# A hybrid decoder layer: the residual row of the last stage added on TensorE instead of VectorE

## The chip, the cores and the metric

The kernel runs on one core of a Trainium2 chip. The metric is the device time of one execution in microseconds. A core has TensorE (PE, matrix products into PSUM), VectorE (DVE), ScalarE (ACT), GpSimd (POOL) and SyncE (SP), each with an instruction stream of its own that it works off in order; they wait for one another by semaphores. Transfers run on DMA queues that SP, ACT and POOL issue to.

## The reference

One inference step of a decoder layer on 1024 new prompt tokens, 16 meta tokens and 8 sampled tokens: linear attention and windowed attention side by side, an output projection with a LayerNorm, and then a mixture of experts with a second LayerNorm. Only the last lines matter for the change:

```python
h1 = layer_norm(ALPHA * h + merged @ w_out, ln1_g, ln1_b)
f = hier_moe(h1...)                  # each token: two experts, weights w_top
#   segment_sum(out[dest] * w_s[:, None])
h2 = layer_norm(ALPHA * h1 + f, ln2_g, ln2_b)

def layer_norm(x, g, b):
    mu = mean(x); var = mean((x - mu) ** 2)
    return (x - mu) * rsqrt(var + LN_EPS) * g + b
```

So for each token the last stage takes its two expert rows, weighs and adds them, adds the row of h1 times ALPHA = 2^0.25, and normalises the sum.

## The kernel before, in words

The tokens stand in NB = 9 blocks of 128 rows and D = 1024 columns. The stages before (projections, attention, output projection, routing) end with the experts: a loop over 32 tiles of 128 gathered rows, each with its expert's weights loaded, split into a high and a low part and multiplied (L1915 to L1917). ACT writes each result tile (yb) to obuf_dram (L1333, L1335).

The last stage begins when the last of these stores has landed. All engines run through blocks 0 to 8 in order, each with its own code:

- POOL gathers for each block the two expert rows of each token, ya and yc, from obuf_dram (L1006), 18 indirect DMAs. Later it adds ln2_b to each block (L1012).
- ACT makes for each block two diagonal matrices dg, the identity scaled by the token's two weights (L1351, L1352). Later, for each block, it makes the reciprocal root of the variance (L1019, L1021) and the normalised row (L1358).
- PE multiplies dg with ya and yc, which weighs each row and adds both in PSUM (L2269, L2270): four products of 512 columns a block. Block b writes the two banks 2*(b % 4) and the next, so PSUM holds four blocks. Before block b it waits for f_z of block b-4 (L2266).
- DVE, in f_sum(b), forms zz = ALPHA * h1 + PSUM (L1887, it sets f_z), then the statistics of zz (L555, L556, L558). f_scale(b-1) multiplies the block before by ln2_g (L1899), and f_mean(b) makes the shift for ACT (L1894). This is the order in its stream.
- SP loads h1 of blocks 0 to 5 into h1l long before, of blocks 6 to 8 into h1e once the experts' memory is free (both L808), and stores each finished block.

h1l and h1e hold the rows of h1; PS is PSUM; zz and st2 have two buffers each. upto(n) is the value that a step's semaphore has once step n is done; f_h[b] is the semaphore of block b's load of h1, f_y[b % 4] that of its gathers, f_dg that of the diagonal matrices (it shares its semaphore with n_whi), n_xn that of the normalised rows, n_hg that of the scaled ones.

Of the kernel before, what the change touches and what calls it, by code (L numbers as in the profile page):

```python
# [31 lines left out]
ACT = mybir.ActivationFunctionType  # L32
ALU = mybir.AluOpType
# [3 lines left out]
P = 128  # L37
# [3 lines left out]
NB = 9  # L41
# [6 lines left out]
ALPHA = 2.0 ** 0.25  # L48
# [18 lines left out]
def upto(n):  # L67

    return n + 1 + CREDIT


def build(nc, A, R):
    ctx = ExitStack()

    def sem(name):
        return ctx.enter_context(nc.semaphore(name))
# [3 lines left out]
    def ssem(name):  # L80
        s = sem(name)
        step_sems.append(s)
        return s
# [13 lines left out]
    def sb(stack, name, shape, dt=F32):  # L97
        return stack.enter_context(nc.sbuf_tensor(name, shape, dt))

    both = ctx  # L100
    PS = ctx.enter_context(nc.psum_tensor("PS", [P, 8, 512], F32))
    ident = sb(both, "ident", [P, P])
# [50 lines left out]
    bias = sb(sW, "bias", [P, 2, HPG, 2 * P])  # L153
# [125 lines left out]
    h1l = sb(sE, "h1l", [P, NB - 3, D])  # L279
# [4 lines left out]
    sF = ExitStack()  # L284
    ya = sb(sF, "ya", [P, NB, D])
    yc = sb(sF, "yc", [P, NB, D])
    h1e = sb(sF, "h1e", [P, 3, D])
    zz = [sb(sF, f"zz{s}", [P, D]) for s in range(2)]
    st2 = [sb(sF, f"st2{s}", [P, 16]) for s in range(2)]
    dg = sb(sF, "dg", [P, NB, 2, P])  # L290
    ln2_g = sb(sF, "ln2_g", [P, D])
    ln2_b = sb(sF, "ln2_b", [P, D])
    sF.close()
# [16 lines left out]
    n_sa = ssem("n_sa")  # L310
    n_st = ssem("n_st")
# [3 lines left out]
    n_xn = ssem("n_xn")  # L315
    n_hg = ssem("n_hg")
# [118 lines left out]
    f_h = ((c_in, 32), (c_rin, 64), (c_brow, 16), (b_gn, 160), (b_gk, 32), (s_in, 64), (s_shift, 32), (s_win, 144), (o_small, 96))  # L435
    f_dg, f_s = n_whi, n_wlo
    f_base = 21
    f_z = ssem("f_z")

    BF = lambda t: t.bitcast(F32)  # L440
    most, rest = slice(1, NB), slice(0, 1)
# [16 lines left out]
    def wait_apart(eng, s, value):  # L458


        if not isinstance(value, int):
            value = eng.to_reg(value)
        eng.wait_ge(c_id, 3)
        eng.wait_ge(s, value)
# [88 lines left out]
    def stats(dve, z, t, s_a, s_b, n):  # L553

        dve.bn_stats(t[:, 0:6], z[:, 0:512])  # L555
        dve.bn_stats(t[:, 6:12], z[:, 512:1024]).then_inc(s_a, 1)  # L556
        wait_apart(dve, s_a, n)
        dve.bn_aggr(t[:, 12:14], t[:, 0:12]).then_inc(s_b, 1)  # L558
# [457 lines left out]
    def _(act):  # L1016
        def rsqrt(src, tmp, dst, s_a, s_b, n, scale=1.0):

            act.activation(tmp, src, ACT.Ln, bias=eps_c[0:src.shape[0], :], scale=scale).then_inc(s_a, 1)  # L1019
            act.wait_ge(s_a, n)  # L1020
            act.activation(dst, tmp, ACT.Exp, scale=-0.5).then_inc(s_b, 1)  # L1021
# [328 lines left out]
        def f_diag(b):  # L1350
            act.activation(dg[:, b, 0], ident[:], ACT.Copy, scale=wts[:, b, 0:1])  # L1351
            act.activation(dg[:, b, 1], ident[:], ACT.Copy, scale=wts[:, b, 1:2]).then_inc(f_dg, 1)  # L1352

        def f_norm(b, s):
            act.wait_ge(n_st, upto(2 * NB + b))
            rsqrt(st2[s][:, 13:14], st2[s][:, 14:15], st2[s][:, 15:16], n_ln, n_rs, upto(2 * NB + b))
            act.wait_ge(n_nm, upto(2 * NB + b))
            act.activation(zz[s][:], zz[s][:], ACT.Identity, bias=st2[s][:, 14:15], scale=st2[s][:, 15:16]).then_inc(n_xn, 1)  # L1358

        for b in range(NB):  # L1360
            f_diag(b)
        for b in range(NB):
            f_norm(b, b % 2)
# [3 lines left out]
    def _(dve):  # L1367
# [513 lines left out]
        def f_sum(b, s):  # L1881

            dve.wait_ge(f_s, f_base + b + 1)
            dve.wait_ge(f_h[b][0], f_h[b][1] + 16)
            dve.wait_ge(n_hg, upto(2 * NB + b - 2))
            q = 2 * (b % 4)
            dve.scalar_tensor_tensor(zz[s][:], h1l[:, b] if b < NB - 3 else h1e[:, b - NB + 3], ALPHA, PS[:, q:q + 2].rearrange("p a n -> p (a n)"),  # L1887
                                     ALU.mult, ALU.add).then_inc(f_z, 1)
            dve.wait_ge(f_z, upto(b))
            stats(dve, zz[s], st2[s], n_sa, n_st, upto(2 * NB + b))  # L1890

        def f_mean(b, s):
            dve.wait_ge(n_rs, upto(2 * NB + b))
# [3 lines left out]
        def f_scale(b, s):  # L1897
            dve.wait_ge(n_xn, upto(2 * NB + b))
            dve.tensor_tensor(ya[:, b], zz[s][:], ln2_g[:], ALU.mult).then_inc(n_hg, 1)  # L1899

        f_sum(0, 0)
        f_mean(0, 0)
        dve.wait_ge(f_small, 32)
        for b in range(1, NB):
            f_sum(b, b % 2)
            f_scale(b - 1, 1 - b % 2)
            f_mean(b, b % 2)
# [4 lines left out]
    def _(pe):  # L1912
# [188 lines left out]
        for a in range(8):  # L2101
            if a >= 2:
                pe.wait_ge(act_s, a - 1)
            for m in range(4):
                g, n = (4 * a + m) // NS, (4 * a + m) % NS
# [20 lines left out]
        for g in range(G):  # L2126
            for h in range(HPG):
                c = (g % 2) * DV + h * HD
# [131 lines left out]


        pe.wait_ge(m_ya, upto(2 * iters + 1))
        for b in range(NB):
            pe.wait_ge(f_dg, f_base + b + 1)
            pe.wait_ge(f_y[b % 4], 32 * (b // 4 + 1))
            pe.wait_ge(f_z, upto(b - 4))  # L2266
            for half in range(2):
                c = slice(half * 512, half * 512 + 512)
                pe.matmul(PS[:, 2 * (b % 4) + half], dg[:, b, 0], ya[:, b, c], start=True, stop=False)  # L2269
                last = pe.matmul(PS[:, 2 * (b % 4) + half], dg[:, b, 1], yc[:, b, c], start=False, stop=True)  # L2270
            last.then_inc(f_s, 1)

    ctx.close()

# [36 lines left out]
```

## Time and profile before

| | |
|---|---|
| median of 3 runs | 1925.24 us (1923.21 to 1931.18) |
| the profiled execution | 1924.17 us, its span 1922.0 us |
| PE, DVE, ACT, POOL busy | 1731.5, 1219.6, 884.9, 306.0 us |
| last expert product ends | about 1850.5 us |
| first product of the last stage | 1866.78 us |
| DVE's first step in it | 1872.95 us |

The span is the time from the first to the last instruction in one profiled execution. Times in a timeline are us from its start. PEclk is the TensorE clock that was granted: 1.00 is 2.4 GHz and 0.50 is 1.2 GHz. A product of f32 operands runs as two passes, so it appears as two weight loads and two matmuls in the trace. Of the 1922 us the last stage takes the last 70 or so.

### The profile page before, as it was taken

The numbers are of one execution on the slowest core, as the hardware profiler recorded it, in microseconds if no ns is written. First come the engines' busy times: TensorE is split into PE (matmuls) and PEld (weight loads), VectorE is DVE, ScalarE is ACT, GpSimd is POOL, SyncE is SP. The second block draws the span as 40 slices with busy tenths as digits, with TensorE's granted clock in tenths as the row PEclk, the third lists the DMA queues.
The fourth block names the chain that finished last, engine by engine and source line by source line (L and its number), as shares of the span: only waits on it lengthen the run. The fifth ranks groups of instructions, "written<-read, shape, count | busy, mean of one in ns | idle before, by whom it ended". The sixth has DMA issues, their size and how long they took to land. (4 is left out here: it accounts for less than half of the span.)

```text
span 1922.0 us, 28799 instructions
## 1 busy us (share of the span) xinstructions
PE 1731.5 (90%) x9022; PEld 1461.6 (76%) x9022; DVE 1219.6 (63%) x1695; ACT 884.9 (46%) x1446; POOL 306.0 (16%) x386
## 2 busy tenths in 40 slices
PE   2899999899999999999978899359999999999955
PEld 2899999788788878878846787348888888888832
DVE  5510110577778767867753333859889988988917
ACT  2432221344445435433411122237787778778723
POOL 1200000122312322232210111010001000010025
PEclk9999999899999999999967899579999999999978
DMA  6486521434433433432269324369999999999854
GB/s 212 147 253 198 177 82 50 146 102 131 142 106 124 135 121 101 158 102 86 84 204 326 122 98 187 119 242 388 413 415 411 415 413 412 416 414 411 328 215 194
DMA packets 183313, 422.90 MB, mean 220 GB/s; under 512 B 24977, under 2 KB 123169, under 8 KB 158425
## 3 DMA queue, kind: packets, MB, share of 16 engines
q1 hardware_dynamic: 129776, 321.93, 45.2%
q0 software_dynamic: 20048, 69.06, 10.2%
q10 hardware_dynamic: 33408, 30.94, 4.6%
q8 instruction: 39, 0.64, 0.1%
q14 instruction: 42, 0.34, 0.1%
HBM read 354.83 MB, written 78.55 MB: 225 GB/s over the span
## 5 line engine op out<-in xcount | busy, mean ns | idle before, releaser
L1786 DVE TENSOR_TENSOR wm_lo<-raw,wm_hi 128x2048 fp32r<-128x2048 f32 x192 | 434.2, 2290 | 72.0 <-ACT wm_hi L1293 70.9
L1293 ACT CAST wm_hi<-raw 128x2048 fp32r<-128x2048 f32 x192 | 363.4, 1911 | 72.8 <-PE PS L1917 44.5
L1915 PE MATMUL PS<-w_hi,hT_hl 128*128 128x512 f32 (+1 forms) x584 | 232.9, 399 | 11.9 <-DMA hT_hl<-hl_dram 8.5
L1916 PE MATMUL PS<-w_lo,hT_hl 128*128 128x512 f32 (+1 forms) x584 | 227.0, 389 | 0.0
L1917 PE MATMUL PS<-w_hi,hT_hl 128*128 128x512 f32 (+1 forms) x584 | 226.6, 388 | 0.0
L1915 PE MATMUL PS<-wm_hi,xT_hi 128*128 128x512 f32 x512 | 203.9, 398 | 2.9 <-DVE xT_lo L1848 2.9
L1917 PE MATMUL PS<-wm_hi,xT_lo 128*128 128x512 f32 x512 | 200.8, 392 | 0.0
L1916 PE MATMUL PS<-wm_lo,xT_hi 128*128 128x512 f32 x512 | 200.5, 392 | 0.0
L1955 PE MATMUL PS<-xa_hi,wn 128*128 128x384 f32 x480 | 161.8, 337 | 0.2
L1957 PE MATMUL PS<-xa_hi,wn 128*128 128x384 f32 x480 | 161.1, 336 | 0.0
L1956 PE MATMUL PS<-xa_lo,wn 128*128 128x384 f32 x480 | 161.1, 336 | 0.0
L1408 DVE TENSOR_TENSOR wn<-nraw,wn 128x1024 fp32r<-128x1024 f32 x20 | 24.5, 1226 | 180.3 <-ACT wn L1040 180.3
L1915 PEld LDWEIGHTS PS<-w_hi,hT_hl 128*128 128x128 f32 x584 | 110.7, 190 | 35.1 <-issue 13.1
L1917 PEld LDWEIGHTS PS<-w_hi,hT_hl 128*128 128x128 f32 x584 | 110.6, 189 | 24.9
L1916 PEld LDWEIGHTS PS<-w_lo,hT_hl 128*128 128x128 f32 x584 | 111.0, 190 | 21.7
L1561 DVE RECIPROCAL Rt<-Et 128x512 f32<-128x512 f32 x36 | 120.7, 3353 | 3.2
L1189 ACT ACTIVATE Sc<-Sc,nmx 128x256 f32<-128x256 f32 (+1 forms) x144 | 69.9, 487 | 109.1 <-DVE nmx L1537 72.5
L1915 PEld LDWEIGHTS PS<-wm_hi,xT_hi 128*128 128x128 f32 x512 | 97.2, 190 | 22.8 <-DVE xT_lo L1848 2.8
L1917 PEld LDWEIGHTS PS<-wm_hi,xT_lo 128*128 128x128 f32 x512 | 96.8, 189 | 21.0
L1916 PEld LDWEIGHTS PS<-wm_lo,xT_hi 128*128 128x128 f32 x512 | 97.0, 189 | 19.6
L1061 ACT COPY ev<-PS 128x384 f32<-128x384 f32 x60 | 28.7, 479 | 171.8 <-PE PS L1957 168.6
L1915 PE MATMUL PS<-wm_hi,hT_hi 128*128 128x512 f32 x256 | 103.0, 403 | 4.5 <-DVE hT_lo L1866 4.5
(340 smaller groups left out, 3387.4 us busy)
## 6 DMA issues: line engine op xcount, KB each, us to landing
raw<-in_w_gate SPq DMA_DIRECT2D x64, 1024.0 KB, 6.9
raw<-in_w_up SPq DMA_DIRECT2D x64, 1024.0 KB, 7.9
raw<-in_w_down SPq DMA_DIRECT2D x64, 1024.0 KB, 8.5
hT_hl<-hl_dram POOLq DMA_DIRECT2D x70, 512.0 KB, 5.4
braw<-in_w_in SPq DMA_DIRECT2D x16, 1024.0 KB, 6.3
obuf_dram<-yb ACTq DMA_DIRECT2D x32, 512.0 KB, 8.2
nd_dram<-ev ACTq DMA_DIRECT2D x72, 192.0 KB, 2.7
nd<-nd_dram SPq DMA_DIRECT2D x36, 384.0 KB, 3.8
```

Source lines behind the costliest of these rows:

```text
L1061: act.copy(ev[k % 3][:], PS[:, 3 + m % 3, 0:T3]).then_inc(n_ev, 1)
L1189: act.activation(Sc[:, h, lo:], Sc[:, h, lo:], ACT.Exp, bias=nmx[:, h:h + 1], accum_out=su[:, h:h + 1])
L1293: act.copy(wm_hi[:, j], raw[:, j]).then_inc(m_hi[j // 4], 1)
L1408: dve.tensor_tensor(lo[:], nraw[r % 3][:], BF(hi[:]), ALU.subtract).then_inc(n_wlo, 1)
L1561: dve.reciprocal(Rt[:], Et[:, 1:3]).then_inc(b_R, 1)
L1786: dve.tensor_tensor(wm_lo[:, j], raw[:, j], BF(wm_hi[:, j]), ALU.subtract).then_inc(m_lo[j // 4], 1)
L1915: pe.matmul(out, x_hi, w_hi_, start=start, stop=False)
L1916: pe.matmul(out, x_hi, w_lo_, start=False, stop=False)
L1917: return pe.matmul(out, x_lo, w_hi_, start=False, stop=stop)
L1955: pe.matmul(out, hi[:, k], xa_hi[:, tc, k], start=(k == 0), stop=False)
L1956: pe.matmul(out, hi[:, k], xa_lo[:, tc, k], start=False, stop=False)
L1957: last = pe.matmul(out, lo[:, k], xa_hi[:, tc, k], start=False, stop=(k == KC - 1))
```

## The change

ALPHA times the row is added by PE: a third diagonal matrix da, the identity times ALPHA, is multiplied with h1l or h1e, ahead of the two products with dg in the same PSUM banks. The rows of blocks 0 to 3 are multiplied ahead of all products with dg; the row of block b+4 directly behind those of block b, after a wait for ACT's normalised row of block b (n_xn). DVE's combination L1887 and its semaphore go. The statistics read PSUM, and so does ACT's normalisation, which then writes zz.

```diff
+    da = sb(sF, "da", [P, P])
...
             act.wait_ge(n_nm, upto(2 * NB + b))
-            act.activation(zz[s][:], zz[s][:], ACT.Identity, bias=st2[s][:, 14:15], scale=st2[s][:, 15:16]).then_inc(n_xn, 1)
-
+            act.wait_ge(n_hg, upto(2 * NB + b - 2))
+            act.activation(zz[s][:], PS[:, 2 * (b % 4):2 * (b % 4) + 2].rearrange("p a n -> p (a n)"), ACT.Identity, bias=st2[s][:, 14:15], scale=st2[s][:, 15:16]).then_inc(n_xn, 1)
+
+        act.activation(da[:], ident[:], ACT.Copy, scale=ALPHA).then_inc(f_dg, 1)
...
             dve.wait_ge(f_s, f_base + b + 1)
-            dve.wait_ge(f_h[b][0], f_h[b][1] + 16)
-            dve.wait_ge(n_hg, upto(2 * NB + b - 2))
             q = 2 * (b % 4)
-            dve.scalar_tensor_tensor(zz[s][:], h1l[:, b] if b < NB - 3 else h1e[:, b - NB + 3], ALPHA, PS[:, q:q + 2].rearrange("p a n -> p (a n)"),
-                                     ALU.mult, ALU.add).then_inc(f_z, 1)
-            dve.wait_ge(f_z, upto(b))
-            stats(dve, zz[s], st2[s], n_sa, n_st, upto(2 * NB + b))
+            stats(dve, PS[:, q:q + 2].rearrange("p a n -> p (a n)"), st2[s], n_sa, n_st, upto(2 * NB + b))
...
         pe.wait_ge(m_ya, upto(2 * iters + 1))
+        def rows(b):
+            pe.wait_ge(f_h[b][0], f_h[b][1] + 16)
+            if b >= 4:
+                pe.wait_ge(n_xn, upto(2 * NB + b - 4))
+            src = h1l[:, b] if b < NB - 3 else h1e[:, b - NB + 3]
+            for half in range(2):
+                pe.matmul(PS[:, 2 * (b % 4) + half], da[:], src[:, half * 512:half * 512 + 512], start=True, stop=False)
+
+        pe.wait_ge(f_dg, f_base + 1)
+        for b in range(4):
+            rows(b)
         for b in range(NB):
-            pe.wait_ge(f_dg, f_base + b + 1)
+            pe.wait_ge(f_dg, f_base + b + 2)
             pe.wait_ge(f_y[b % 4], 32 * (b // 4 + 1))
-            pe.wait_ge(f_z, upto(b - 4))
             for half in range(2):
                 c = slice(half * 512, half * 512 + 512)
-                pe.matmul(PS[:, 2 * (b % 4) + half], dg[:, b, 0], ya[:, b, c], start=True, stop=False)
+                pe.matmul(PS[:, 2 * (b % 4) + half], dg[:, b, 0], ya[:, b, c], start=False, stop=False)
                 last = pe.matmul(PS[:, 2 * (b % 4) + half], dg[:, b, 1], yc[:, b, c], start=False, stop=True)
             last.then_inc(f_s, 1)
+            if b + 4 < NB:
+                rows(b + 4)
```

PE's stream before, at the start of the last stage; each row is one product of 512 columns, with the semaphores that it waits for (n_whi is that of dg):

```order
L2269 MATMUL PS<-ya,dg 128x512 [waits f_y0,f_z,n_whi,m_ya]
L2270 MATMUL PS<-yc,dg 128x512
L2269 MATMUL PS<-ya,dg 128x512
L2270 MATMUL PS<-yc,dg 128x512
L2269 MATMUL PS<-ya,dg 128x512 [waits f_z,f_y1,n_whi]
L2270 MATMUL PS<-yc,dg 128x512
```

PE's stream of the changed kernel, from the last row product of blocks 0 to 3 to the first products of block 1 (b_gk is that of the load of block 4 of h1):

```order
L2266 MATMUL PS<-h1l,da 128x512
L2276 MATMUL PS<-ya,dg 128x512 [waits f_y0,n_whi]
L2277 MATMUL PS<-yc,dg 128x512
L2276 MATMUL PS<-ya,dg 128x512
L2277 MATMUL PS<-yc,dg 128x512
L2266 MATMUL PS<-h1l,da 128x512 [waits n_xn,b_gk]
L2266 MATMUL PS<-h1l,da 128x512
L2276 MATMUL PS<-ya,dg 128x512 [waits f_y1,n_whi]
L2277 MATMUL PS<-yc,dg 128x512
```

A block's products now have two row products behind them that wait for n_xn, ahead of the next block's. The same follows blocks 1 to 4.

DVE's stream before, for block 1:

```order
L1887 SCALAR_TENSOR_TENSOR zz<-h1l,PS 128x1024 [waits c_rin,n_hg,n_wlo,f_small]
L555 BN_STATS st<-zz 128x6 [waits f_z]
L556 BN_STATS st<-zz 128x6
L558 BN_AGGR st<-st 128x2 [waits n_sa,c_id]
L1899 TENSOR_TENSOR ya<-zz,ln_g 128x1024 [waits n_xn]
L1894 SCALAR_TENSOR_TENSOR st<-st 128x1 [waits n_rs]
```

and in the changed kernel (n_wlo is PE's f_s):

```order
L555 BN_STATS st<-PS 128x6 [waits n_wlo,f_small]
L556 BN_STATS st<-PS 128x6
L558 BN_AGGR st<-st 128x2 [waits n_sa,c_id]
L1896 TENSOR_TENSOR ya<-zz,ln_g 128x1024 [waits n_xn]
L1891 SCALAR_TENSOR_TENSOR st<-st 128x1 [waits n_rs]
```

The combination is gone, and the statistics wait for PE themselves; the rest stands in the same order.

## Rows read from the trace of the kernel before

**Rows 1.** The page, busy time: us (share of the span) xinstructions.

```profile
PE 1731.5 (90%) x9022; PEld 1461.6 (76%) x9022; DVE 1219.6 (63%) x1695; ACT 884.9 (46%) x1446; POOL 306.0 (16%) x386
```

**Rows 2.** The chain that ended last, 1845 to 1922 us: start, us, what.

```profile
1856.48 10.06 DMA yc<-obuf_dram,ridx
...
1872.95 1.23 DVE zz L1887
1876.57 1.23 DVE zz L1887
...
1880.65 1.23 DVE zz L1887
...
1905.10 1.23 DVE zz L1887
```

**Rows 3.** Timeline of PE, last stage: start, us, engine line, idle before and releaser.

```profile
1866.78 2.04 PE L2269 MATMUL PS<-ya,dg 128*128 128x512 f32 x2 [16.23 <-DMA yc<-obuf_dram,ridx]
1868.62 1.91 PE L2270 MATMUL PS<-yc,dg 128*128 128x512 f32 x2
...
1871.62 1.02 PE L2270 MATMUL PS<-yc,dg 128*128 128x512 f32 x2
1872.48 1.02 PE L2269 MATMUL PS<-ya,dg 128*128 128x512 f32 x2
```

**Rows 4.** Timeline of DVE and ACT, blocks 0 and 1.

```profile
1874.20 0.69 DVE L555 BATCH_NORM_STATS2 st<-zz 128x6 f32<-128x512 f32 x1
...
1876.59 1.24 ACT L1358 ACTIVATE zz<-zz,st 128x1024 f32<-128x1024 f32 x1 [0.23 <-DVE st L1894]
...
1877.83 0.70 DVE L555 BATCH_NORM_STATS2 st<-zz 128x6 f32<-128x512 f32 x1
...
1879.22 0.21 DVE L558 BATCH_NORM_AGGREGATE st<-st 128x2 f32<-128x12 f32 x1
...
1879.35 1.17 DVE L1899 TENSOR_TENSOR ya<-zz,ln_g 128x1024 f32<-128x1024 f32 x1
...
1880.62 1.24 ACT L1358 ACTIVATE zz<-zz,st 128x1024 f32<-128x1024 f32 x1 [0.63 <-DVE st L1894]
```

**Rows 5.** Stretches: length, busy PE, PEld, DVE, ACT, POOL, PEclk, DMA, GB/s.

```profile
1838.80:1843.10 4.30, 0.00 (x0) 0.00 (x0) 3.82 (x3) 2.71 (x3) 0.00 (x0) 1.00 0.13 53
1843.90:1847.30 3.40, 3.40 (x9) 2.61 (x9) 0.00 (x0) 0.00 (x0) 0.00 (x0) 0.50 0.00 0
1850.70:1854.10 3.40, 0.00 (x0) 0.00 (x0) 0.00 (x0) 2.18 (x2) 0.00 (x0) 1.00 0.38 154
1854.30:1866.70 12.40, 0.00 (x0) 0.00 (x0) 0.00 (x0) 5.36 (x18) 7.49 (x8) 0.50 0.85 322
1866.80:1871.20 4.40, 4.40 (x6) 1.82 (x7) 0.00 (x0) 0.00 (x0) 2.80 (x3) 0.50 1.03 412
```

**Rows 6.** Groups by form that read PSUM, on ACT and DVE: busy, mean ns.

```profile
L1333 ACT COPY yb<-PS 128x1024 f32<-128x1024 f32 x32 | 32.6, 1019 | 9.1 <-PE PS L1917 9.1
L1548 DVE COPY Pt<-PS 128x512 f32<-128x512 f32 x36 | 24.8, 690 | 51.5 <-PE PS L2036 51.5
```

**Rows 7.** Timeline, the end: block 8 on DVE and POOL.

```profile
1906.36 0.69 DVE L555 BATCH_NORM_STATS2 st<-zz 128x6 f32<-128x512 f32 x1
...
1910.42 2.13 DVE L1899 TENSOR_TENSOR ya<-zz,ln_g 128x1024 f32<-128x1024 f32 x1 [1.31 <-ACT zz L1358]
1912.63 2.34 POOL L1012 TENSOR_TENSOR ya<-ya,ln_b 128x1024 f32<-128x1024 f32 x1 [1.16 <-DVE ya L1899]
```

**Rows 8.** The first dg on ACT (timeline), and the loads of h1 (line L808).

```profile
1854.48 0.40 ACT L1351 ACTIVATE dg<-ident,wts 128x128 f32<-128x128 f32 x1 [1.06 <-DMA obuf_dram<-yb]
...
L808 SPq DMA_DIRECT2D h1l<-h_dram x6: 340/433/1077, 1214.6 to 1216.9; - x6
L808 SPq DMA_DIRECT2D h1e<-h_dram x3: 424/432/772, 1855.3 to 1856.3; - x3
```

**Rows 9.** Waits, 1866 to 1915 us: total us, times, longest.

```profile
PE PS L2269 <- DMA yc<-obuf_dram,ridx: 16.2, 1, 16.2
```

## What I predict, and how it is worked out

> **What bounds the kernel now.** I read the page first, then the chain of waits over the last 75 us, then the timelines of PE, DVE and ACT in it. The page shows PE busy for 90% of the span [rows 1], but nearly all of that is the projections and the experts, and the change touches none of it. What decides here is the last stage, after the last expert product at 1850.5 us. The chain [rows 2] shows what ends last in it: the gather of yc lands 10.06 us after its issue began at 1856.48 (1866.54), PE does block 0, and from 1872.95 on every step of the chain is on DVE. The combination of a block (L1887) starts at 1872.95, 1876.57, 1880.65 and so on to the ninth at 1905.10, so 4.08 us apart from block 1 on. PE is not late there: from 1872.48 it issues a product of 512 columns every 0.86 us in two passes of 0.43 [rows 3], four to a block, 3.44 us, less than DVE's 4.08, and it runs ahead by up to four blocks of PSUM.
>
> **What the change does to a block.** On DVE it takes away L1887, 1.23 us of those 4.08 [rows 2]; what is left is 2.85. On PE it adds two products for the scaled row, so 6 products, 12 passes, 12 x 0.43 = 5.16 us a block instead of 3.44. For blocks 0 to 3 these are done ahead of the gathers. For blocks 4 to 8 they stand in PE's stream right behind the products of blocks 0 to 4, and with them a new wait: the row of block b+4 overwrites the banks that ACT's normalisation of block b now reads, so it waits for that normalisation. Before, PSUM was free once L1887 had read it, and the wait (f_z) stood four blocks later than the products that filled the bank. Now the wait for block b's normalisation stands directly behind block b's own products. Behind the waiting row are queued the products of block b+1, whose gathers are long in. DVE waits for those, and ACT and POOL for DVE. So five times the last stage goes round a loop in which nothing overlaps.
>
> **The loop, step by step, at the full clock.**
> - From the start of a block's statistics to the end of its normalisation: in block 1 from 1877.83 to 1880.62 + 1.24 = 1881.86, 4.03 us; in it the aggregate and DVE's scale of block 0 (1.17, ahead of the mean in DVE's stream) [rows 4]. In block 0, with no scale between, 1874.20 to 1877.83, 3.63 us. Both engines now read PSUM. For ACT the nearest rows are its copies of 128x1024 from PSUM at 1.02 us against 1.24 for this one out of SBUF; for DVE a copy of 128x512 from PSUM has 0.69 us [rows 6], as the statistics of 512 have [rows 4]. So I take 0.22 off: 3.81 and 3.41. Bounds: no saving, or 0.22 as taken.
> - The end of ACT to PE's first pass: 0.24, as from the landing at 1866.54 to the first product at 1866.78 [rows 2, 3].
> - Two row products and four of the next block: 12 passes from one another at 0.43, 5.16, plus 0.16 that the last pass lasts beyond its 0.43 (1.02 for two).
> - PE's end to DVE's start: 1871.62 + 1.02 = 1872.64 to 1872.95, 0.31 [rows 2, 3].
>
> That makes 3.81 + 0.24 + 5.16 + 0.16 + 0.31 = 9.68 us for a block that took 4.08.
>
> **The clock.** In such a loop PE stands still for 3.81 + 0.24 + 0.31, 4.4 us, in each round. The trace has one pause of that length in the stage before: none busy from 1838.8 to 1843.1, at the full clock, and then 3.4 us of work at a granted clock of 0.50, which is 1.2 GHz, from 1843.9 to 1847.3. After 3.4 us of standing (1850.7 to 1854.1) it also fell to 0.50, stayed there through the wait for the gathers, and for 4.4 us of work after it [rows 5]. A slow stretch of 3.4 us does 1.7 us of work, so it costs 1.7; I take one such stretch for each round: 11.4 us. The bounds are none (9.68) and the whole burst at 0.50: a product then takes 1.71 us instead of 0.86, as the one at 1868.62 with its two passes of 0.85 [rows 3], so the round takes about 15.0.
>
> The Trainium skill, in "TensorE: Matmul & The Clock Gate", section "HAM oscillation — how this bites in real kernels", says that short bursts of matmuls with waits between them lose the full clock in every wait and start each burst at the low one. The pause at 1838.8 agrees, with 0.50 for 3.4 us behind it. Taken so far that the whole burst is slow, it is the rival "slow throughout" below.
>
> **The start.** The products of the rows of blocks 0 to 3 need da, one more copy on ACT ahead of dg, 0.40 us from 1854.48 [rows 8], and h1l, whose loads are issued by 1216.9 [rows 8]. They run from about 1855.1: 16 passes, 6.9 us at the full clock (1862.0), 13.8 at 0.50 (1868.9). The clock fell at 1854.1, and in the kernel before it came back after 4.4 us of work [rows 5]; so they end near 1864 and are hidden by the gathers, which land at 1866.54. Block 0's products then take 7 x 0.43 + 0.59 to the end of the last pass at the full clock and give DVE its start at 1866.78 + 3.60 + 0.31 = 1870.7; at 0.50 as before, 1872.95. I take 1871.5. The statistics start there, with no L1887 ahead: before, 1874.20 [rows 4]. This is all that the change wins at the start, 2.7 us. The loads of h1e (3, 9.4 to 11.5 us to landing, issued by 1856.3 [rows 8]) are in before the row of block 6 is wanted.
>
> **The end.** Behind block 5 no rows are left, and PE paces at 3.44 a block, DVE's 2.85 being less: three blocks, 10.3 us. From the statistics of block 8 to the end of the span it is 1922.0 - 1906.36 = 15.64; in it is DVE's last scale, which took 2.13 beside POOL's addition, POOL's last addition from 1912.63, and the store [rows 7]. All this stays; ACT's 0.22 comes off: 15.42.
>
> **The sum.** 1871.5 + (11.4 - 0.4) + 4 x 11.4 = 1928.1 for the start of block 5; + 10.3 = 1938.4; + 15.4 = 1953.8, against a span of 1922.0. The profiled execution took 1924.17, 2.17 beyond its span, so 1956.0; it lay 1.07 under the median of 1925.24, which is less than the spread of the runs. I predict 1956, 1.6% slower. Nothing else costs: SP's and POOL's streams are the same, and the dg of block 0 comes 0.3 us later in a wait of 12 us.
>
> **The rivals.**
> - Full clock throughout: the loop is there, but pauses of 4.4 us with 5.2 of work between don't lose the clock. For it: more than half of each round is work, and no row shows such a mixture repeated. Against it: the two falls to 0.50 after 4.3 and 3.4 us without work [rows 5]. Time: 1870.7 + 5 x 9.68 - 0.4 + 10.3 + 15.4 = 1944.4, so 1946.6.
> - Slow throughout: the clock does not come back inside a burst. For it: 4.4 us of work at 0.50 after the long wait [rows 5], nearly a burst. Against it: the 3.4 us stretch, after which PE had 1.00. Time: 1872.95 + 5 x 15.0 - 0.4 + 10.3 + 15.4 = 1973.3, so 1975.4.
> - The wait is not felt (the other side): the rows find their bank free when PE comes to them, because something holds PE back by as much anyway. Place: PE at the row of block 4. It decides from the point where the products of block b+1 would start more than 4.4 us after block b's, thus if gathers came that far apart. Price: then PE's own work paces, 5 x 5.16 + 3 x 3.44 = 36.1 from 1871.5, plus 15.4: 1923.0, so 1925.2, no change. Against it: PE waited for a gather once in this stage, before block 0 [rows 9]. If the rows cost PE nothing at all: 1870.7 + 8 x 3.44 + 15.4 = 1913.6, so 1915.8, the best that the change could do, 0.5% faster.
>
> In the same page of the Trainium skill, the section "Architectural detail: the array is 16× 32×32, not 1× 128×128" says that PE's queue may pull a weight load ahead of matmuls in flight. If that reached past the waiting row, it would hide 0.2 us a round at most; the products themselves would still stand behind it. No row here shows either.
>
> **How the numbers follow.** Forecast 0.63, full clock 0.17, slow throughout 0.15, the wait not felt 0.05. The forecast's own range is 1951 to 1964 (one to one and a half slow stretches, and the bounds of the start). The range takes in the full-clock case and two thirds of the way to the slow one: 1945 to 1969. What a measurement tells from no change is 0.5%, 9.6 us: slower means over 1934.9, which all cases but the last give, 0.95; the same 0.04; faster 0.01.
>
> **What would show it.** In the profile after: PE idle five times for about 4.4 us at the row products, with ACT's normalisation as the releaser; DVE's first statistics 11 to 12 us apart over blocks 0 to 5 and about 3.4 over 5 to 8; ACT's normalisation near 1.02; the clock at 0.50 for a part of each burst; eight row products done before the gathers land. Wrong would be: statistics evenly 5.2 us apart (no wait felt), 9.7 (full clock) or 15 (slow), or a time below 1935.

## The result

| | median, us | runs | ratio to before |
|---|---|---|---|
| before, at the time | 1924.22 | 4 | |
| changed | 1959.22 (1954.91 to 1964.01) | 4 | 1.0192 [1.0154, 1.0230] |

The change costs 1.9% by the ratio, 35 us between the medians. The forecast was 1956, 1.6% slower, with 1945 to 1969 for the range. The profiled execution of the changed kernel took 1960.57 with a span of 1958.7.

### The profile page after: what moved, and what is told of

The parts are those of the page before. It is cut to its first block and busy times, and to the rows that moved or that the text cites. A ratio compares the mean times of both kernels' runs of the same rounds, so it can differ in the third digit from the quotient of the medians.

```text
span 1958.7 us, 28867 instructions
## 1 busy us (share of the span) xinstructions
PE 1764.8 (90%) x9058; PEld 1476.6 (75%) x9058; DVE 1209.2 (62%) x1686; ACT 884.5 (45%) x1447; POOL 306.4 (16%) x386
```

## The profile after

Waits of the changed kernel from 1866 to 1955 us (us in total, times, longest). Before, PE waited in this stage only once, for a gather [rows 9]:

```profile
DVE st L555 <- PE PS L2277: 76.7, 9, 29.3
...
PE PS L2266 <- ACT zz L1359: 20.7, 5, 4.3
...
PE PS L2276 <- DMA yc<-obuf_dram,ridx: 2.0, 1, 2.0
```

The second row is the loop: five waits of the row products (L2266) for ACT's normalisation, 20.7 us. DVE's waits for PE are the other side of it.

Timeline of PE, the first two rounds and the last of the five, to answer to [rows 3]:

```profile
1855.90 10.01 PE L2266 MATMUL PS<-h1l,da 128*128 128x512 f32 x16 [4.34 <-issue]
1867.92 1.40 PE L2276 MATMUL PS<-ya,dg 128*128 128x512 f32 x2 [2.01 <-DMA yc<-obuf_dram,ridx]
1869.12 1.91 PE L2277 MATMUL PS<-yc,dg 128*128 128x512 f32 x2
...
1872.27 1.02 PE L2277 MATMUL PS<-yc,dg 128*128 128x512 f32 x2
1877.17 3.75 PE L2266 MATMUL PS<-h1l,da 128*128 128x512 f32 x4 [3.88 <-ACT zz L1359]
1880.72 1.78 PE L2276 MATMUL PS<-ya,dg 128*128 128x512 f32 x2
...
1884.06 1.02 PE L2277 MATMUL PS<-yc,dg 128*128 128x512 f32 x2
1889.33 3.52 PE L2266 MATMUL PS<-h1l,da 128*128 128x512 f32 x4 [4.25 <-ACT zz L1359]
...
1924.13 3.75 PE L2266 MATMUL PS<-h1e,da 128*128 128x512 f32 x4 [4.19 <-ACT zz L1359]
```

The 16 passes of the early rows take 10.0 us and end 2.0 us ahead of the gathers: hidden, as the second row's wait shows. Then PE stands for 3.9 to 4.25 us ahead of each burst of rows and products. The four passes of a block's two row products take 3.5 to 3.75 us, about twice the 1.88 of the full clock (row_late, below).

Timeline of DVE and ACT, one round (block 1), to answer to [rows 4]:

```profile
1885.18 0.70 DVE L555 BATCH_NORM_STATS2 st<-PS 128x6 f32<-128x512 f32 x1 [9.39 <-PE PS L2277]
...
1886.71 1.17 DVE L1896 TENSOR_TENSOR ya<-zz,ln_g 128x1024 f32<-128x1024 f32 x1
...
1887.98 1.20 ACT L1359 ACTIVATE zz<-PS,st 128x1024 f32<-128x1024 f32 x1 [0.63 <-DVE st L1891]
...
1896.32 0.70 DVE L555 BATCH_NORM_STATS2 st<-PS 128x6 f32<-128x512 f32 x1 [8.37 <-PE PS L2277]
```

From 1885.18 to 1887.98 + 1.20 = 1889.18 are 4.00 us, and PE starts 0.15 later. The first statistics of the nine blocks start at 1873.43, 1885.18, 1896.32, 1908.71, 1919.98, 1932.48, 1935.92, 1939.35 and 1942.78: rounds of 11.75, 11.14, 12.39, 11.27 and 12.50, then 3.44, 3.43 and 3.43. Before it was 4.08 a block.

Stretches of the changed kernel, pauses and bursts in turn (length, busy PE, PEld, DVE, ACT, POOL, PEclk, DMA, GB/s), to answer to [rows 5]:

```profile
1885.20:1889.30 4.10, 0.00 (x0) 0.00 (x1) 2.65 (x5) 1.70 (x3) 1.27 (x1) 0.97 0.56 224
1889.40:1896.30 6.90, 6.88 (x12) 2.73 (x12) 0.00 (x0) 0.00 (x0) 0.97 (x1) 0.78 0.03 5
1896.40:1900.40 4.00, 0.00 (x0) 0.00 (x0) 2.58 (x5) 1.70 (x3) 1.30 (x1) 0.86 0.00 0
1900.50:1908.70 8.20, 8.17 (x12) 3.22 (x12) 0.00 (x0) 0.00 (x0) 0.94 (x1) 0.66 0.16 64
```

Twelve passes take 6.9 us in one burst and 8.2 in the next, for 5.2 at the full clock. The granted clock is at one of its two levels at any moment, so a mean of 0.78 or 0.66 is a burst that begins at 0.50 and ends at 1.00: the row products at its head last 3.5 to 3.75 us, the products with dg at its end 1.02.

The times of one kernel spread by up to 14 us (row_late: 1922.32 to 1936.03), so I use a second measure of the traces beside the times: the length of the last stage, from the first product with dg to the start of POOL's last addition. Before it is 1912.63 - 1866.78 = 45.9 us [rows 3, 7], after 1949.30 - 1867.92 = 81.4. The difference of 35.5 is the whole loss. The kernel before ran again beside the experiments: its median was 1927.61 beside the first four and 1927.88 beside the next three, and their ratios are to those runs.

## Experiments

The theory: PE stands because the row of block b+4 waits, in order, for the normalisation of block b, behind block b's own products; the pause costs by itself, and again by the low clock after it. The rivals: the ten added products cost; the reads of PSUM cost; the low clock is the whole cost.

### The same products, moved (row_late)

```diff
         for b in range(NB):
+            if b >= 4:
+                rows(b)
             pe.wait_ge(f_dg, f_base + b + 2)
...
             last.then_inc(f_s, 1)
-            if b + 4 < NB:
-                rows(b + 4)
```

> The changed kernel with one thing moved: the row product of block b (b = 4 to 8) stands directly ahead of block b's own products instead of behind block b-4's. Same 54 products, same waits by value. The wait theory: the normalisation of block b-4 is done by then, so PE never stops; DVE's first statistics come 3.4 us apart for blocks 1 to 3 and 5.2 for blocks 4 to 8, 36 us in all from block 0 to block 8 instead of 69.4, and the time falls by 33 us to about 1926. Rival, the added products (or reading PSUM) cost by themselves: the time stays near 1950 to 1959.

Measured: 1926.75 median, ratio to before 1.0004 [0.9983, 1.0024]. Timeline of PE, blocks 3 to 5:

```profile
1877.96 1.02 PE L2279 MATMUL PS<-yc,dg 128*128 128x512 f32 x2
1878.82 1.88 PE L2266 MATMUL PS<-h1l,da 128*128 128x512 f32 x4
1880.54 1.02 PE L2278 MATMUL PS<-ya,dg 128*128 128x512 f32 x2
...
1883.97 1.88 PE L2266 MATMUL PS<-h1l,da 128*128 128x512 f32 x4
```

No pause is left, all at the full clock, and a block takes 1883.97 - 1878.82 = 5.15 us. From the first statistics (1868.82) to those of block 8 (1904.78) are 36.0 us. Before they were 1906.36 - 1874.20 = 32.2 [rows 4, 7], so this takes 3.8 us longer; 1.9 of them come back at the start, where the statistics begin 5.5 us after the first product with dg instead of 7.4. The last stage is 1911.05 - 1863.32 = 47.7 us, 1.9 more than before. So with every added product and every read of PSUM in place, 1.9 of the 35.5 us are left, and the place of the rows costs 81.4 - 47.7 = 33.7. Even with no pause the full change gains nothing.

### The wait without the products (wait_only)

This kernel leaves ALPHA * h1 out of blocks 4 to 8.

```diff
-            for half in range(2):
+            for half in range(2 if b < 4 else 0):
                 pe.matmul(PS[:, 2 * (b % 4) + half], da[:], src[:, half * 512:half * 512 + 512], start=True, stop=False)
...
-                pe.matmul(PS[:, 2 * (b % 4) + half], dg[:, b, 0], ya[:, b, c], start=False, stop=False)
+                pe.matmul(PS[:, 2 * (b % 4) + half], dg[:, b, 0], ya[:, b, c], start=(b >= 4), stop=False)
```

> The changed kernel without the row products of blocks 4 to 8 (their rows of h1 are left out of the sum), but with their waits in the same places. The wait theory: PE still stops for block b's normalisation behind block b; a round is shorter only by its two products, 1.7 us (at the full clock) of 11.8, so five times 1.7 to 2.6: 1946 to 1951. Rival, the added products cost: it falls to the time of the kernel before, about 1924.

Measured: 1951.58, 0.6 us above the range that I gave, ratio 1.0126 [1.0089, 1.0162]; last stage 1941.14 - 1871.48 = 69.7 us, 11.7 less than the changed kernel. The wait without its products makes 24 of the 35.5 us. Waits, 1870 to 1945 us:

```profile
PE PS L2276 <- issue: 20.5, 5, 4.2
```

The five pauses add up to 20.5 us beside 20.7, though the trace names no releaser for them here. The 11.7 us are more than five times 1.7 (8.6), which the ten products take at the full clock. The other 3.1 are slow work that is gone. The clock didn't fall in every pause here. Timeline of PE, the first burst and the head of the fourth:

```profile
1880.68 1.10 PE L2276 MATMUL PS<-ya,dg 128*128 128x512 f32 x2 [3.84 <-issue]
1881.62 1.02 PE L2277 MATMUL PS<-yc,dg 128*128 128x512 f32 x2
...
1883.33 1.02 PE L2277 MATMUL PS<-yc,dg 128*128 128x512 f32 x2
...
1907.59 2.05 PE L2276 MATMUL PS<-ya,dg 128*128 128x512 f32 x2 [4.14 <-issue]
```

The first burst stands behind a pause of 3.84 us and ran wholly at the full clock (granted clock 1.00); the fourth, behind 4.14 us, had a mean of 0.57. Why one pause loses the clock and another of nearly its length doesn't, no run here settles.

### PE kept at work in the pause (warm)

nul is a matrix of zeros, so its products add 0 to banks that are already being summed, and the result is unchanged.

```diff
+        act.activation(nul[:], ident[:], ACT.Copy, scale=0.0)
         act.activation(da[:], ident[:], ACT.Copy, scale=ALPHA).then_inc(f_dg, 1)
...
             if b + 4 < NB:
+                for half in (0, 1, 0, 1):
+                    pe.matmul(PS[:, 2 * ((b + 1) % 4) + half], nul[:], h1l[:, 0, half * 512:half * 512 + 512], start=False, stop=False)
                 rows(b + 4)
```

> The changed kernel with four extra products by a matrix of zeros (they add 0 to the next block's banks) ahead of each of the five waits, so that PE works in the 4.3 us in which it otherwise stands: 3.4 us of work at the full clock. The clock theory: the 2.0 us by which a round is longer than its steps at the full clock (11.8 measured, 9.8 from the steps) is the low clock after each pause; with PE busy the rounds shrink to about 9.8 and the time falls by 10 to about 1949. Rival, the low clock doesn't come from the pause, or zeros don't count as work: no change in the clock, and the extra products take 6.9 us at 0.50, so the rounds grow to 14 and the time to 1970.

Measured: 1952.14, ratio 1.0131 [1.0092, 1.0170]; last stage 1939.64 - 1869.78 = 69.9 us, 11.5 less. Three of its rounds as stretches (columns as above), and the wait in them:

```profile
1878.70:1888.30 9.60, 8.82 (x20) 3.72 (x20) 2.66 (x5) 1.66 (x4) 3.74 (x4) 1.00 1.03 410
1888.30:1897.90 9.60, 8.82 (x20) 3.72 (x20) 2.66 (x5) 1.73 (x4) 2.44 (x2) 1.00 0.10 35
1897.90:1907.50 9.60, 8.82 (x20) 3.72 (x20) 2.66 (x5) 1.73 (x4) 2.37 (x2) 1.00 0.14 56
```

```profile
1893.90 3.60 PE L2283 MATMUL PS<-h1l,nul 128*128 128x512 f32 x8
1898.25 1.95 PE L2268 MATMUL PS<-h1e,da 128*128 128x512 f32 x4 [0.75 <-ACT zz L1360]
```

With the clock at 1.00 a round is 9.6 us. The products by zeros kept the clock up. So of the 81.4 - 45.9 = 35.5 us, the low clock after the pauses is 11.5, a third; PE works longer and the kernel gets faster. The other two thirds, 24 us, are the serial loop at the full clock: five rounds of 9.6 in place of 4.08, less what the start and the last three blocks (3.44 in place of 4.08) give back.

### The wait in the kernel before (before_wait)

```diff
             pe.wait_ge(f_z, upto(b - 4))
+            if 1 <= b <= 5:
+                pe.wait_ge(n_xn, upto(2 * NB + b - 1))
```

> The kernel before with nothing but a wait added on PE: the products of blocks 1 to 5 wait for the normalisation of the block ahead of them. No added product, no read of PSUM. The wait theory: a round is 1.2 + 4.0 + 0.2 + 3.4 + 0.5 = 9.4 us at the full clock and about 11.1 with one slow stretch, in place of 4.08, five times: 1951 to 1959. Rival, the products or the reads of PSUM make the loss: close to 1924.

Measured: 1963.97, ratio 1.0197 [1.0160, 1.0233], last stage 1952.02 - 1869.41 = 82.6 us. Without a single added product and with the statistics out of SBUF, the wait alone makes the whole loss. It came out 5 us above the upper end that I gave; 3.4 of them are the kernel before, at 1927.61 in this series and 1924.22 when I worked out the range. Waits, 1869 to 1955 us:

```profile
PE PS L2271 <- ACT zz L1358: 21.9, 4, 5.5
```

The fifth pause, ahead of block 1, is 5.3 us; the trace puts it down to a gather, but PE starts 0.14 us after ACT's first normalisation ends (1880.50 and 1880.36). A pause is longer than the changed kernel's, since DVE's combination stands in it. That makes 6.1 us of the difference to wait_only, where the wait cost 24; another 3.8 are the start and the last three blocks, which are as slow here as before (7.3 us to the first statistics, 4.08 a block). Blocks 1 to 3 start their combination at 1885.93, 1898.13 and 1909.35, 12.2 and 11.2 apart, more than the 11.1 that one slow stretch for each round gives.

### One block later (row_one_later)

```diff
             last.then_inc(f_s, 1)
-            if b + 4 < NB:
-                rows(b + 4)
+            if b and b + 3 < NB:
+                rows(b + 3)
```

> The changed kernel with the row products of block b+4 behind the products of block b+1 instead of block b's: one block later. The wait theory: the normalisation of block b ends 4.0 us after its statistics begin, and a block's products take 3.4, so only the first of the five waits still shows (0.5 us or so), and the time is that of the version with the rows directly ahead of their block, 1927 (ratio 1.00), 32 us under the changed kernel. Rival, what that version gained was distance from the gathers or from ACT's queue, so one block is not enough: the waits stay for a part, and the time lies near the middle, 1940.

Measured: 1930.28, ratio 1.0023 [1.0009, 1.0037]; last stage 1916.63 - 1868.06 = 48.6 us. Timeline of PE, the first two rows in the stream:

```profile
1877.31 1.95 PE L2266 MATMUL PS<-h1l,da 128*128 128x512 f32 x4 [0.45 <-ACT zz L1359]
...
1882.54 1.88 PE L2266 MATMUL PS<-h1l,da 128*128 128x512 f32 x4
```

One wait of 0.45 is left of five. Moving each row by one block gives back 32.8 of the 33.7 us of last stage that moving it as far as it goes gives. The stage is 2.7 us longer than before; the ratio says 0.23% slower, with 0.09 to 0.37% for its interval (1.7 to 7 us).

### Only the rows that are free (early_rows_only)

Rows of blocks 0 to 3 as in the changed kernel; blocks 4 to 8 combined on DVE as before.

```diff
+    ON_PE = (0, 1, 2, 3)
...
+            if b in ON_PE:
+                stats(dve, PS[:, q:q + 2].rearrange("p a n -> p (a n)"), st2[s], n_sa, n_st, upto(2 * NB + b))
+                return
...
+            dve.scalar_tensor_tensor(zz[s][:], h1l[:, b] if b < NB - 3 else h1e[:, b - NB + 3], ALPHA, PS[:, q:q + 2].rearrange("p a n -> p (a n)"),
+                                     ALU.mult, ALU.add).then_inc(f_z, 1)
+            dve.wait_ge(f_z, upto(b - 4))
+            stats(dve, zz[s], st2[s], n_sa, n_st, upto(2 * NB + b))
```

> Rows of blocks 0 to 3 on PE, done in the wait for the gathers, with statistics and normalisation out of PSUM; blocks 4 to 8 on DVE as before, with no row product in PE's stream. If DVE is the only bound left in blocks 0 to 3: 1.2 us less for each and one less at the start, about 4 us less than before (ratio 0.998). If DVE's scale and POOL's addition of ln2_b can't run at once (in the version with late rows one scale lasted 3.33 us beside POOL's 2.36), a block can't be shorter than 1.17 + 2.35 = 3.5 us once POOL adds, and 1 us is left (ratio 0.9995).

Measured: 1925.44, ratio 0.9990 [0.9973, 1.0006], not told from before; last stage 1914.20 - 1870.38 = 43.8 us, 2.0 shorter than before, between the two cases that I gave. What came between shows in the timeline of POOL and DVE:

```profile
1884.48 4.67 POOL L1014 TENSOR_TENSOR ya<-ya,ln_b 128x1024 f32<-128x1024 f32 x2
1885.91 4.33 DVE L1907 TENSOR_TENSOR ya<-zz,ln_g 128x1024 f32<-128x1024 f32 x1
1890.16 0.15 DVE L1902 SCALAR_TENSOR_TENSOR st<-st 128x1 f32<-128x1 f32 x1
1890.32 2.37 POOL L1014 TENSOR_TENSOR ya<-ya,ln_b 128x1024 f32<-128x1024 f32 x1 [1.17 <-DVE ya L1907]
1890.37 1.22 DVE L1895 SCALAR_TENSOR_TENSOR zz<-h1l,PS 128x1024 f32<-128x1024 f32 x1
```

POOL had the first two blocks to add one behind the other. A scale of 1.17 us took 4.33: it began during the first addition and ended 1.09 us after the second (1889.15). The combination L1895, with one operand in PSUM, ran beside POOL's next one in its 1.22.

### The last row too, and zeros ahead of the start (early_rows_and_last)

```diff
+    ON_PE = (0, 1, 2, 3, 8)
...
         for b in range(4):
             rows(b)
+        for half in (0, 1) * 1:
+            pe.matmul(PS[:, half], nul[:], h1l[:, 0, half * 512:half * 512 + 512], start=False, stop=False)
...
+            if b >= 4:
+                if b in ON_PE:
+                    rows(b)
```

> As the version with early rows only, and the row of block 8 on PE too, directly ahead of its products, where PE is ahead of DVE; and two products by zeros between the last early row and the gathers, so that PE doesn't stand for 2 us there. Expected: block 0's products at the full clock, 1.7 us earlier than without them, and DVE's last combination gone (1.2 us): 2 to 4 us less than before (ratio 0.998 to 0.999), the best of all versions. Rival: POOL's additions, which can't run beside DVE's scales, set the end: then neither shows, and it is the time of the version before it.

Measured: 1923.89, ratio 0.9983 [0.9967, 0.9999]; last stage 1912.03 - 1868.78 = 43.3 us, 2.6 shorter than before. It has the lowest median of all versions, by less than 0.2%; against early_rows_only its stage is 0.5 us shorter, and the times don't tell the two apart. The start is at the full clock:

```profile
1866.84 1.88 PE L2290 MATMUL PS<-h1l,nul 128*128 128x512 f32 x4
1868.78 1.10 PE L2301 MATMUL PS<-ya,dg 128*128 128x512 f32 x2
```

DVE's first statistics start at 1872.58, 3.8 us after the first product with dg; in the changed kernel it was 1873.43 - 1867.92 = 5.5. That the zeros did this isn't shown: early_rows_only has none, its PE stood for 1.6 us, and its start was at the full clock too, with the statistics (1874.18) 3.8 us after the first product:

```profile
1870.38 1.10 PE L2297 MATMUL PS<-ya,dg 128*128 128x512 f32 x2 [1.61 <-DMA yc<-obuf_dram,ridx]
```

The 1.7 us that I expected from the zeros, against the version with early rows only, did not come.

### POOL's addition cut short (short_pool_add)

This is early_rows_and_last with one more edit. It leaves ln2_b out of 1016 of the 1024 columns.

```diff
-            pool.tensor_tensor(ya[:, b], ya[:, b], ln2_b[:], ALU.add).then_inc(n_h, 1)
+            pool.tensor_tensor(ya[:, b, 0:8], ya[:, b, 0:8], ln2_b[:, 0:8], ALU.add).then_inc(n_h, 1)
```

> The version with early rows and the last one, with POOL adding ln2_b to 8 of the 1024 columns of each block only (the bias is left out for the rest). If POOL's 2.35 us additions hold up DVE's scales: the scale that lasted 4.33 us falls to 1.17 and the last one from 2.1 to 1.17, and from the first product with dg to the start of POOL's last addition it takes 39.1 us instead of 43.25. Rival, the long scales are something else (the gathers' traffic, or ACT reading PSUM at the same time): they stay, and the stage is not shorter.

Measured once: 1914.62 beside 1930.14 of the kernel before, a pair too few to weigh by its times; last stage 1905.22 - 1866.29 = 38.9 us, for 39.1 expected. The line of DVE's scale, count, duration ns min/median/max, first in the version with the full addition, then in this one:

```profile
L1909 DVE TENSOR_TENSOR ya<-zz,ln_g x9: 1171/1171/4328, 1877.5 to 1909.8; 128x1024 f32<-128x1024 f32 x9
```

```profile
L1909 DVE TENSOR_TENSOR ya<-zz,ln_g x9: 1171/1172/1226, 1875.0 to 1903.9; 128x1024 f32<-128x1024 f32 x9
```

No scale is held any more, and the stage is 4.4 us shorter than with the full addition. So in the versions with early rows it is POOL's addition that eats most of what DVE saves.

## Why the prediction was right

The steps, each with what it measured:

- The place of the wait. Right: five pauses with ACT's normalisation as the releaser. row_late, which moves only that place, takes 33.7 us of the stage away, and before_wait, which adds only the wait, makes a loss of that size.
- The round at the full clock, 9.68. Measured 9.6 in warm, where the clock held. Three terms in it were off and nearly cancel, which is luck: ACT's normalisation out of PSUM takes 1.20, not 1.02 (out of SBUF 1.24 [rows 4]; the plain copy [rows 6] was the wrong row to take it from); from ACT to PE it is 0.15, not 0.24; and from PE's last pass to DVE 0.10 (1884.06 + 1.02 to 1885.18), not 0.31. ACT's normalisation near 1.02 was one of the signs that I named, and it failed.
- The clock, 1.7 a round. Too small: the five rounds sum to 59.05 and at 9.6 would be 48.0, less 0.4 for the first; so it is 2.3 a round. The mean granted clock of two bursts was 0.78 and 0.66, so 3.0 and 5.6 us of them were at 0.50; I had taken a stretch like the shorter of these for all, from the one pause in the trace before. "Full clock throughout" and "slow throughout" are both out.
- The start. I took 4.7 us from the first product with dg to the first statistics; it was 5.5. The early rows were hidden as forecast (end 2.0 us ahead of the gathers), but the clock fell once more in block 0 (the product at 1869.12 has passes of 0.85). Against before, the statistics come 1.9 us sooner after the first product with dg (5.5 for 7.4), not 2.7.
- The blocks after the fifth, 3.44: measured 3.44, 3.43, 3.43. The end, 15.42 from block 8's statistics: measured 1958.7 - 1942.78 = 15.9.
- The sum. The span of this execution is 4.9 us over the forecast span of 1953.8. The five rounds make 2.5 of them (59.05 for 56.6), the start 0.8, the end 0.5, and 1.1 lies ahead of the stage, whose first product with dg came at 1867.92 and not at 1866.78. This execution was 1.3 slower than the median, so the forecast misses the median by 3.2.
- "The wait is not felt": for this placement false. Its time, worked out as 1925, is that of row_late, 1927: there PE paces five blocks at 5.15 for DVE's 4.08, and the faster start and the other three blocks give about that much back.

The rule that I cited from the Trainium skill ("TensorE: Matmul & The Clock Gate", section "HAM oscillation — how this bites in real kernels"), that bursts with waits between them start cold again and again, holds here in all five rounds, and warm shows it by the counter-test: 11.5 us. It isn't without exception: in wait_only one burst of five, behind a pause of 3.84 us, ran at the full clock.

The weight load that the prediction let run ahead of the wait did not: in the changed kernel it begins at 1877.14, 0.03 us before the row product that waited (1877.17).

## What to carry to other kernels

When work is added to an engine whose stream is in order, look at what its wait waits for and where that stands: a prefetch into a buffer that the current step still uses must stand at least one step's chain later in the stream, or everything behind it waits too. When the last reader of a buffer moves to a later step, the buffer is held for longer, here from the end of DVE's one read (1.2 us) to the end of statistics and normalisation (4.0 us). Price a pause of PE twice, once for itself and once for the slow work after it.

## What the runs showed of the hardware

- DVE's product of two SBUF tensors and POOL's addition don't run at once (early_rows_only, short_pool_add); DVE's combination with one operand in PSUM does. The Trainium skill has this in "GPSIMD Engine Reference", section "1. Specifications": POOL shares SBUF interfaces with VectorE and contends with DVE instructions that have two SBUF inputs. The trace agrees, and shows the DVE instruction held until POOL's operations end, the one in progress and the one queued directly behind it (4.33 us for 1.17).
- Products by a matrix of zeros held the granted clock at 1.00 through pauses in which it otherwise fell (warm: 1.00 in rounds of 9.6 us; the changed kernel: means of 0.78 and 0.66 in the bursts behind the pauses).
- DVE's statistics take 0.70 out of PSUM and 0.70 out of SBUF; ACT's normalisation 1.20 and 1.24.
